# A hybrid-layer kernel: lookups summed by halves, a skip product moved in POOL's order, a store waited for later, residual rows in other buffers

## The reference, cut to what matters

```python
def ssd_scan(...):                    # 32 heads in 8 groups, 5 chunks of 128 tokens
    scores = einsum(C, B)             # per chunk
    y_diag = einsum(scores * decay_in, xdt)
    y_off  = einsum(C, prev_state, exp(a_cs))
y = y_f + flip(y_b) + d_skip[:, None] * xs          # the skip term
y = rmsnorm(y.reshape(...) * silu(z), ssd_norm_w)

def peer(x, w_pq, sub_keys, u_tab, v_tab):           # 8 heads, 16 experts each
    top_s, top_i = top_k(s, 16)                      # for two halves of the key
    best_s, pos = top_k(top_s[..., 0, :, None] + top_s[..., 1, None, :], 16)
    idx  = take_along_axis(cand_i, pos)              # the routing lookup
    gate = softmax(best_s)
    act  = gelu(einsum('td,thkd->thk', x, u_tab[idx]))
    return einsum('thk,thkd->td', gate * act, v_tab[idx])

x = x + gate2 * peer(h, ...)                         # residual
y = rmsnorm(x, final_norm_w)
```

## Time and profile before

| | us |
|---|---|
| median of 3 runs | 3030.18 |
| lowest and highest | 3029.78, 3034.5 |
| the profiled execution | 3027.34 |
| its span | 3025.6 |
| mean granted TensorE clock | 0.934 |
| PE, DVE, ACT, POOL busy | 2618.1, 2236.7, 1046.5, 697.2 |

### The profile page before, as it was taken

The page is one execution under the profiler, slowest core; times in us unless marked ns, Lnnn a source line. Parts: engine busy times, 40 slices in busy tenths (PEclk is TensorE's granted clock), DMA queues, the critical chain, the costliest instruction groups (busy, mean ns, idle before and its releaser), DMA issues. The chain is left out here.

```text
span 3025.6 us, 40625 instructions
## 1 busy us (share of the span) xinstructions
PE 2618.1 (87%) x15117; PEld 2280.5 (75%) x15117; DVE 2236.7 (74%) x3784; ACT 1046.5 (35%) x1515; POOL 697.2 (23%) x582
## 2 busy tenths in 40 slices
PE   4979999998899999598785238799999999999995
PEld 3967777777777777398685238698999999898984
DVE  2556666662476677523479999599999999999997
ACT  3224444442243333221332138333333333333332
POOL 0000000000365566100000038232323232323230
PEclk7989999999899999799897669899999999999997
DMA  6421112112323222332211005899999999999994
GB/s 253 169 103 46 60 46 77 53 52 102 124 72 121 72 87 78 134 150 91 105 42 42 14 41 238 346 410 410 399 404 397 403 398 403 398 401 400 400 402 193
DMA packets 147402, 615.36 MB, mean 203 GB/s; under 512 B 13104, under 2 KB 72272, under 8 KB 84432
## 3 DMA queue, kind: packets, MB, share of 16 engines
q1 hardware_dynamic: 110128, 345.26, 30.5%
q0 software_dynamic: 36864, 268.45, 21.6%
q10 hardware_dynamic: 288, 0.03, 0.0%
HBM read 557.29 MB, written 56.41 MB: 203 GB/s over the span
## 5 line engine op out<-in xcount | busy, mean ns | idle before, releaser
L2076 POOL DMA_INDIRECT p_uv<-in_uv_rows,merged x256 | 331.0, 1293 | 736.3 <-DVE merged L2228 660.6
L2090 PE MATMUL p_pa<-h2D,w_hi 128*128 128x384 f32 x1024 | 345.7, 338 | 9.5 <-PEq L2309 8.8
L2092 PE MATMUL p_pa<-h2D,w_lo 128*128 128x384 f32 x1024 | 345.3, 337 | 0.0
L2091 PE MATMUL p_pa<-h2D,w_hi 128*128 128x384 f32 x1024 | 345.1, 337 | 0.0
L2228 DVE SCALAR_TENSOR_TENSOR merged<-p_uv,p_sw,merged 128x1024 f32<-128x1024 f32 x256 | 328.9, 1285 | 9.2
L2127 ACT ACTIVATE w_hi<-w_raw 128x2048 fp32r<-128x2048 f32 x126 | 241.5, 1917 | 267.2 <-PE p_py L2106 246.8
L2214 DVE CUSTOM_DVE_ANT_0 p_uv<-p_uv,merged 128x1024 f32<-128x1024 f32 x256 | 307.3, 1219 | 14.7 <-DMA p_uv<-in_uv_rows,merged 14.7
L2104 PE MATMUL p_py<-w_hi,p_wh 128*128 128x512 f32 x768 | 303.9, 396 | 6.7 <-DVE w_lo L2192 6.7
L2192 DVE TENSOR_TENSOR w_lo<-w_raw,w_hi 128x2048 fp32r<-128x2048 f32 x126 | 288.5, 2289 | 27.8 <-ACT w_hi L2127 27.7
L105 DVE TENSOR_TENSOR w_lo<-w_raw,w_hi 128x2048 fp32r<-128x2048 f32 x64 | 150.7, 2356 | 208.4 <-ACT w_hi L100 208.2
L2105 PE MATMUL p_py<-w_lo,p_wh 128*128 128x512 f32 x768 | 303.5, 395 | 0.0
(11 more groups left out here) (351 smaller groups left out, 5972.5 us busy)
## 6 DMA issues: line engine op xcount, KB each, us to landing
w_raw<-in_w_stream SPq DMA_DIRECT2D x190, 1024.0 KB
g_dram<-e_st SPq DMA_DIRECT2D x6, 4096.0 KB, 11.3
p_g<-g_dram SPq DMA_DIRECT2D x64, 384.0 KB
t_ada<-in_w_ada SPq DMA_DIRECT2D x16, 1024.0 KB, 10.1
xc_dram<-c_xc SPq DMA_DIRECT2D x8, 1284.0 KB, 4.5
s_xx<-xc_dram SPq DMA_DIRECT2D x8, 642.0 KB, 6.0
s_bc<-xc_dram SPq DMA_DIRECT2D x8, 642.0 KB, 8.0
gate_dram<-s_gst SPq DMA_DIRECT2D x16, 320.0 KB, 5.2
```

What stands on the lines that cost most here:

```text
L2076: nc.gpsimd.indirect_dma_start(uv[:, k % RING, :], None, K.uv_rows, bass.IndirectOffsetOnAxis(K.sidx[:, t, c:c + 1], 0)).then_inc(K.gather ...
L2090: nc.tensor.matmul(ps_a[m][:, :], wh[:, k, cols], K.h2D[0][:, k, :], start=k == 0, stop=False)
L2091: nc.tensor.matmul(ps_a[m][:, :], wh[:, k, cols], K.h2D[1][:, k, :], start=False, stop=False)
L2092: mm = nc.tensor.matmul(ps_a[m][:, :], wl[:, k, cols], K.h2D[0][:, k, :], start=False, stop=k == KD - 1)
```

## The change

Four edits. In the scan, POOL's skip product moves from behind `rT` to the end of the slot, behind A. In routing, `eq` and `fr` become one buffer each for both key halves; one product covers both, and the sum over 16 candidates is made by halves: three 16-bit sums over 8, 4 and 2 candidates and a last one that writes the 32-bit slots. In the gates phase SP no longer waits for its last stores; in the experts phase SP, POOL and ACT wait for them ahead of their first use of that memory. At the end, the residual rows go to five other places: tile 0 to `K.hrow`, in the midst of the expert loop (SP's loop is cut at 18), where POOL multiplies its sum with the gate and adds it after gather 160; tiles 1 to 4 to the halves of the two `w_raw` buffers, loaded when the last weight split is done.

```diff
@@ phase_ssd, gpsimd
-                if b is not None:
-                    skip(b)
                 g, k = (q - 2) // NT, (q - 2) % NT
                 if 0 <= g < GROUPS:
                     carry(g, k)
...
                 if b is not None:
                     forward_part(b)
+                    skip(b)
@@ phase_route, vector
-                stage([nc.vector.tensor_tensor(eq[c][:, :, :, :], eq[c][:, :, :, :], fr[c][:, :, :, :], ALU.mult)
-                       for c in range(2)])
+                found = eq[:, :, :, :, :].rearrange("p c t e k -> p (c t) (e k)")
+                stage([nc.vector.tensor_tensor(found, found, fr[:, :, :, :, :].rearrange("p c t e k -> p (c t) (e k)"), ALU.mult)])
+                for n in (8 * TOPK, 4 * TOPK, 2 * TOPK):
+                    stage([nc.vector.tensor_tensor(found[:, :, 0:n], found[:, :, 0:n], found[:, :, n:2 * n], ALU.add)])
                 dve.wait_ge(be_done, h + 1)
-                stage([nc.vector.tensor_reduce(sm[:, :], be[:, :, :], axis=AX.X, op=ALU.add)]
-                      + [nc.vector.tensor_reduce(slots[:, c, :, slot], eq[c][:, :, :, :].rearrange("p t e k -> p t k e"), axis=AX.X, op=ALU.add) for c in range(2)])
+                pair = found.rearrange("p (c t) n -> p c t n", c=2)
+                stage([nc.vector.tensor_reduce(sm[:, :], be[:, :, :], axis=AX.X, op=ALU.add),
+                       nc.vector.tensor_tensor(slots[:, 0:2, :, slot], pair[:, :, :, 0:TOPK], pair[:, :, :, TOPK:2 * TOPK], ALU.add)])
@@ phase_gates, sync
-            for s in range(2):
-                sp.wait_ge(out[s], 16 * (BLOCKS // 2))
@@ phase_experts: the same wait at the start of sync, gpsimd and scalar
+            for s in range(2):
+                sp.wait_ge(K.g_out[s], 16 * (TD // TB // 2))
@@ phase_experts, sync
-            with sp.Fori(0, 30) as i:
+            with sp.Fori(0, 18) as i:
+                pair(2 * i, 0)
+                pair(2 * i + 1, 1)
+            sp.wait_ge(dot_done, SLOTS)
+            sp.dma_start(res[0], K.x2_dram[0:P, :]).then_inc(res0_in, 16)
+            with sp.Fori(18, 30) as i:
...
-            sp.wait_ge(v_done, NTS * SLOTS)
-            sp.dma_start(res, K.x2_dram.rearrange("(t p) d -> p t d", p=P)).then_inc(res_in, 16)
+            sp.wait_ge(K.w_lo_done, U_EXP + 2 * PAIRS)
+            for t in range(1, NT):
+                sp.dma_start(res[t], K.x2_dram[t * P:(t + 1) * P, :]).then_inc(res_in, 16)
@@ phase_experts, gpsimd
+                if k == 160:
+                    pool.wait_ge(row_in, 48)
+                    pool.wait_ge(res0_in, 16)
+                    nc.gpsimd.tensor_tensor(ys[:, 0, :], ys[:, 0, :], gate2[:, group(0), :], ALU.mult).then_inc(gated0, 1)
+                    pool.wait_ge(gated0, 1)
+                    nc.gpsimd.tensor_tensor(res[0], res[0], ys[:, 0, :], ALU.add).then_inc(summed0, 1)
@@ phase_experts, vector
-            dve.wait_ge(res_in, 16)
+            dve.wait_ge(res_in, 16 * (NT - 1))
...
-                if t < NT:
+                if 1 <= t < NT:
                     residual(t)
```

More of the change, by code:

```diff
@@ L1716, in phase_route @@
     name = sb("r_name", [P, 2, TOPK]); names = sb("r_names", [P, 2, TOPK, TOPK], BF16)
-    eq = [sb(f"r_eq{i}", [P, NT, TOPK, TOPK], BF16) for i in range(2)]
-    fr = [sb(f"r_fr{i}", [P, NT, TOPK, TOPK], BF16) for i in range(2)]; f_done = sem("r_f_done"); fr_done = sem("r_fr_done"); bs = sb("r_bs", [P, NT, TOPK]); be = sb("r_be", [P, NT, TOPK])
+    eq = sb("r_eq", [P, 2, NT, TOPK, TOPK], BF16)
+    fr = sb("r_fr", [P, 2, NT, TOPK, TOPK], BF16); f_done = sem("r_f_done"); fr_done = sem("r_fr_done"); bs = sb("r_bs", [P, NT, TOPK]); be = sb("r_be", [P, NT, TOPK])
     sm = sb("r_sm", [P, NT])
@@ L1808, in replicas @@
                 for c in range(2):
-                    nc.scalar.activation(fr[c][:, :, :, :], f16[:, :, c, :].unsqueeze(3).to_broadcast([P, NT, TOPK, TOPK]), ACT.Copy).then_inc(fr_done, 1)
+                    nc.scalar.activation(fr[:, c, :, :, :], f16[:, :, c, :].unsqueeze(3).to_broadcast([P, NT, TOPK, TOPK]), ACT.Copy).then_inc(fr_done, 1)
             def gate_exp(h):
@@ L1881, in search @@
                 slot = slice(TOPK * h, TOPK * (h + 1))
-                stage([nc.vector.tensor_tensor(eq[c][:, :, :, :], kc[:, c, :, :].unsqueeze(2).to_broadcast([P, NT, TOPK, TOPK]),
+                stage([nc.vector.tensor_tensor(eq[:, c, :, :, :], kc[:, c, :, :].unsqueeze(2).to_broadcast([P, NT, TOPK, TOPK]),
                                                names[:, c, :, :].unsqueeze(1).to_broadcast([P, NT, TOPK, TOPK]), ALU.is_equal)
@@ L1930, in phase_gates @@
     hot_done = sem("e_hot"); weighted = sem("e_weighted"); mm_done = sem("e_mm"); ev_done = sem("e_ev")
-    out = [sem("e_out0"), sem("e_out1")]
+    out = K.g_out
     with nc.Block() as block:
@@ L2019, in phase_experts @@
     gate2 = sb("p_g2", [P, 2, D]); norm_w = sb("p_nw", [P, D]); ss = sb("p_ss", [P, NT])
-    res = uv[:, 0:3, :].rearrange("p a d -> p (a d)")[:, 0:NT * D].rearrange("p (t d) -> p t d", t=NT)
+    res = [K.hrow[:, 0, :], K.raw[1][:, D:2 * D], K.raw[0][:, 0:D], K.raw[0][:, D:2 * D], K.raw[1][:, 0:D]]
     fin = uv[:, 3:6, :].rearrange("p a d -> p (a d)")[:, 0:NT * D].rearrange("p (t d) -> p t d", t=NT)
@@ L2030, in phase_experts @@
     r_done = sem("p_r"); o_done = sem("p_o"); out = sem("p_out")
+    res0_in = sem("p_res0_in"); gated0 = sem("p_gated0"); summed0 = sem("p_summed0")
     with nc.Block() as block:
@@ L2071, in _ @@
         def _(pool):
+            for s in range(2):
+                pool.wait_ge(K.g_out[s], 16 * (TD // TB // 2))
             for k in range(NTS * SLOTS):
@@ L2144, in slot_gelu @@
                 nc.scalar.activation(sg[:, GS * s:GS * s + GS], sa[:, GS * s:GS * s + GS], ACT.Gelu_apprx_tanh).then_inc(sg_done, 1)
+            for s in range(2):
+                act.wait_ge(K.g_out[s], 16 * (TD // TB // 2))
             gelu(0, 0)
@@ L2176, in _ @@
                 if t < NT:
-                    act.wait_ge(summed, t + 1)
+                    if t:
+                        act.wait_ge(summed, t)
+                    else:
+                        act.wait_ge(summed0, 1)
                     if t:
                         act.wait_ge(sq_done, t)
-                    nc.scalar.activation(sq, res[:, t, :], ACT.Square, accum_out=ss[:, t:t + 1]).then_inc(sq_done, 1)
+                    nc.scalar.activation(sq, res[t], ACT.Square, accum_out=ss[:, t:t + 1]).then_inc(sq_done, 1)
                 if t:
@@ L2263, in residual @@
                         nc.vector.tensor_tensor(fin[:, t, cols], ps_y[2 * (t - NTS) + d][:, :], gate2[:, group(t), cols], ALU.mult).then_inc(scaled, 1)
-                dve.wait_ge(scaled, 2 * t + 2)
-                nc.vector.tensor_tensor(res[:, t, :], res[:, t, :], fin[:, t, :], ALU.add).then_inc(summed, 1)
+                dve.wait_ge(scaled, 2 * t)
+                nc.vector.tensor_tensor(res[t], res[t], fin[:, t, :], ALU.add).then_inc(summed, 1)
             def mean_square(t):
@@ L2356, in build @@
                            for i, d in enumerate((U32, F32)))
+        K.g_out = [sem("g_out0"), sem("g_out1")]
         K.gathered = [sem(f"gathered{b}") for b in range(RING)]
```

4 lines of the change are left out of this document (2 added, 2 removed).

## The result

The changed kernel takes 2992.58 us (median of 4 runs, 2992.27 to 2992.9) against 3030.09 before; the ratio is 0.9871, with a 95% interval of 0.9857 to 0.9886. That is 37.5 us saved, where 47.8 were forecast, and 2992.6 where 2982.4 stood. The range, 2973.0 to 2995.4, holds it.

What follows compares the result with a forecast made beforehand. Bounds: TensorE in experts and, with gaps, scan; DVE in routing; DVE behind a DMA at the end. 22.0 + 13.0 + 1.7 + 11.6 - 0.5 = 47.8 us saved, 3030.18 to 2982.4 us; range 2973 to 2995.

Steps and rivals of the forecast that it cites:

- Routing: Routing stage: sums by halves at the 16-bit pace save 2.75 us per head, 22 us over 8 heads.
- rival (a): Routing: the halving sums run at the 32-bit pace; 38.4 us saved, 2991.8 us; chance 0.11.
- (b): Scan gives nothing: POOL's wait moves behind A with `rT` late, or M waits for ACT's E; 2995.4 us; chance 0.15.
- (d): Scan: skip and `rT` run beside DVE's sums, making M late in 28 more steps; slower, 3146 us; chance 0.03.
- The end: Kernel's end: DVE starts tile 1's residual at 2991.4 instead of 3003.00, without a DMA wait; 11.6 us saved.
- 7.0 + 8.3 less about 2 for smaller waits that reappear: Scan: PE's waits for M, plus time at low clock, less new waits; 13 us saved, bounds 5 and 18.
- The three falls of the earlier trace: Scan: low-clock stretches after three late-A waits of PE, 8.3 us lost, expected to go with those waits.
- The start of the experts: Expert stage's opening: gathers move 2.1 us earlier, SP's loads by less; 1.7 us saved, bounds 0 and 4.
- 0 to 3.8, taken as 0.5: Expert loop: cost of POOL's two instructions after gather 160, 1.90 us each, with DVE losing up to 1.9 us.
- rival (c): Expert stage: PE waits because DVE loses its lead to POOL, end rows land late; +3.3 +1.5, 2987.2 us; no separate chance.
- a rival that did not come true: The case of no gain in the scan, 2995.4 us, which set the range's upper end; chance 0.15.

Runs made afterwards that it cites:

- e5_rt_late: Changed kernel with POOL's `rT` built behind the state products and a wait for DVE's `xs` of the same slot; 2978.51 us.
- e6_half_rt: Changed kernel with the second of `rT`'s two products left out from step 2 on; one run, 2982.89 us.
- e2_skip: Kernel before with only the skip product moved behind A; 3020.41 us, ratio 0.9958.
- e7_pieces: Changed kernel with POOL's gating and residual of tile 0 cut into eight pieces of 128 columns, behind gathers 160 to 216; 2987.58 us.
- e8_rows_late: Changed kernel with the three row loads (1.5 MB) moved from the expert stage's opening to behind rounds 12, 24 and 36; 2990.31 us.
- e10_changed: The changed kernel itself, measured again on the chip of its variants; 2992.35 us, ratio 0.9869 to the kernel before.
- e11_dve0: Changed kernel with tile 0 finished on DVE behind the last take, no POOL work behind gather 160; one run, 2988.41 us.
- e9_together: Changed kernel with `rT` behind DVE's `xs`, tile 0 in eight pieces, row loads behind rounds 12, 24 and 52; 2970.27 us.

## Why the prediction was right, and where it was not

**Routing, right.** The view that mattered was the product with `fr`: same inputs, same type, in place. Its pace of 0.52 ns an element held for all three sums, down to rows of 32 elements, and rival (a) falls. So do (b) and (d): the scan gave 9.6 us, neither nothing nor a loss.

**The end, right**, to 0.3 us. The four loads did pay for their starts, some 0.9 us against the proportion, but that hid behind the last takes, and PE's last matmul hid behind tile 1.

**The scan, right in sign and mechanism, too large by 3.4 us.** The step that failed is the term "7.0 + 8.3 less about 2 for smaller waits that reappear". DVE's wait for A and PE's wait for M came out as forecast (40.7 and 12.8 us; about 40 and 14 were named). The waits for M fell by 8.9 us, where 7.0 were counted. The reappearing waits were mis-sized: they are 6.0 us, at `s_pst` (11.3 - 5.3), where 2 were counted. So PE's idle time fell by 3.0 and not by 5.0, and the new waits brought two falls of the clock of their own. They come from a step that I dealt with in one sentence. I asked of `rT` only when PE needs its result, and that was never in question. I did not ask what would run beside it. Against rival (d) I wrote that POOL's doubling of DVE's sums is in the rows already. It was in the rows of another instruction: the sum lost half of it (1396 to 1017 ns) and `xs` took on more (537 to 843 ns), from `rT` and from the state products, which moved up with the skip gone. The Trainium skill (GPSIMD Engine Reference, Key points), which I cited there, says that GpSimd contends with instructions of VectorE that have two SBUF inputs; e5_rt_late and e6_half_rt agree, with 14.6 and 9.3 us of the scan, and in e5_rt_late the instructions that read PSUM kept their 0.69 and 0.42 us beside `rT`. What I drew from it was too weak: not how often they meet, but which instruction of DVE is the one that is met.

**The clock, partly.** The three falls of the earlier trace rows went with their waits, as forecast, 8.3 us. But two others appeared, each behind a pair of short waits (1.02 or 1.04, and 0.82 us) with one matmul group between them, so the busy time of PE in the scan fell by 6.6 only, and 1.3 of that stem from the end of the scan and not from these falls. Which pairs bring a fall differs from one execution to the next. In the six with this order of the scan (the changed kernel, e2_skip, e7_pieces, e8_rows_late, e10_changed, e11_dve0) the clock fell once or twice between 800 and 1200 us, near 870, 1062 or 1170, and the scan took 458.1 to 459.3 us. The Trainium skill (TensorE: Matmul & The Clock Gate, Part 1) says that one kernel may leave the low rate at different points from run to run. It says so of a kernel's start; in these six it is the falls in the midst that come at different points, at a price of about 1 us between them. With the short waits gone, in e5_rt_late and e9_together, and with fewer of them, in e6_half_rt, no fall was left between 800 and 1190 us.

**The start of the experts, wrong.** I moved the gathers by 2.1 us and took 1.7 of it for the path. They moved by 1.3 (from 17.1 to 15.8 us behind the last gates matmul), and the stretch to round 2 gained 0.3 or nothing. I wrote that this stretch is bound by the DMA and then counted an earlier issue as a gain. e8_rows_late shows what does count there: 1.5 MB fewer gave 4.2 us.

**Inside the experts, wrong by 2.5 us.** The term "0 to 3.8, taken as 0.5" should have been 3.0, or some 4.6 where the clock falls behind the stall. Its two numbers were both too low: POOL's instructions took 6.0 us, not 3.8, because DVE slows them as they slow DVE, and DVE lost 4.2 us, not up to 1.9. And DVE's loss was set against its spare time over the whole stage (36 us in 1000), although it came in one round, which has 0.6 us to spare. The rival (c) had this mechanism with its 3.3 us, and the range held it.

**What is left.** 3.4 + 1.4 + 2.5 + 0.3 - 0.9 = 6.7 us by stages. The other 3.5 up to the 10.2 that are missing by the medians can't be placed: a median has no stages. The stages without an edit scatter by that much from one execution to another, and no run separates it further. That the total stayed inside the range owes something to its width, 22 us: its upper end is the price of a rival that did not come true, and the measured time lies 3 us below it.
